# New distances between the moving tiles and the weight blocks in four feed-forward layers

## The chip, the cores and the metric

The program runs on one core of a Trainium2 chip. The metric is the device time of one execution in microseconds; three executions of the kernel before gave 2782.95, 2782.99 and 2783.01 us, median 2782.99 us.

## The reference

Two blocks of a transformer-like network run one after the other on 256 tokens of width 1024. The first block has two layers with a Fourier and a retention mixer; the second has two layers (`l` = 0, 1), each a feed-forward network (ffn), a mixer of state-space, pooling and attention parts, and another ffn. The change is about the four ffns of the second block:

```python
def _swiglu(x, w_gate, w_up, w_down):   # the ffn: 1024 -> 2816 -> 1024
    return (silu(x @ w_gate) * (x @ w_up)) @ w_down
...
    for l in range(DEPTH):
        f = _swiglu(_rmsnorm_2(h, ff1_norm_pre[l]), ff1_w_gate[l], ff1_w_up[l], ff1_w_down[l])
        h = h + 0.5 * _rmsnorm_2(f, ff1_norm_post[l])
        ...
        f = _swiglu(_rmsnorm_2(h, ff2_norm_pre[l]), ff2_w_gate[l], ff2_w_up[l], ff2_w_down[l])
        h = h + 0.5 * _rmsnorm_2(f, ff2_norm_post[l])
```

## The kernel before

All matrix products are made in float32 accuracy out of three products in the faster fp32r type: an operand is split into a high part (rounded to fp32r) and a low part (what was left), and w_hi·hi, w_hi·lo and w_lo·hi are added up in PSUM. `pe_block` (L1182) issues the three matmuls; they are L1193, L1194 and L1195 of every profile row below. Each loads its own block of 128 x 128 weights (PEld, LDWEIGHTS) and then streams a moving tile of 256 token columns (512 in most of the first block) through it.

The weights come from HBM in units of 512 KB into a ring of four slots, `raw` (SP's queue issues them). ACT copies a unit to `w_hi` (`split_hi`, L727), DVE subtracts to get `w_lo` (`split_lo`, L736), and PE consumes the unit. A plan made when the program is built gives each unit its slot; PE waits for `lo_ready` before a unit and counts it off in `unit_used` behind it.

An ffn of the second block (`ffn`, L369) has five steps. "gain" scales the stream `h` into the moving tiles `u_hi` (ACT, `act_gain`, L1688) and `u_lo` (DVE, `dve_gain_tile`, L1695). "up" is a Gemm of 11 turns of 96 matmuls on `u_hi`, `u_lo`; ACT and DVE make g = silu(gate) * up out of it and split it into `g2_hi` (L1080) and `g2_lo` (L1143). "down" is a Gemm of 528 matmuls on `g2_hi`, `g2_lo`. "stats" and "post" normalize and add to `h`. The first two turns of "up" have waits in them, since the token norm is worked out meanwhile; from the third turn to the end of "down", 9 x 96 + 528 = 1392 matmuls, the engine has all it needs ahead of it. This is called the long stretch of an ffn below.

**Where the operands lie.** A partition of SBUF is a row of bytes, and the program lays its buffers one behind another in it. `u_hi`, `u_lo`, `raw`, `w_hi` and `w_lo` follow each other, and each is a whole number of 256 bytes long (4160, 4160, 4 x 1056, 4 x 1088 and 4 x 1088 floats), so they all start at the same place modulo 256. A weight block starts at a multiple of 512 bytes in its slot of 4352 bytes = 17 x 256, so every weight block is at that place too. A moving tile of 256 columns is not:

```python
SHIFT, ROOM = 48, 64
...
        def tokens_at(n, wide=False):
            at = SHIFT if n == SEQ and not wide else 0
            return slice(at, at + n)
```

`tokens_at` (L613) puts it 48 floats, 192 bytes, behind. `g2_hi` and `g2_lo` are in an overlay that starts with `tables` and `poolw` (L461 to 463) and come to the same 192. The distance of the moving tile behind the weight block modulo 256 is called the distance here. The kernel has others too:

- distance 0: the Gemms "q" and "gate" of the retention mixer (`both=True`, 256 columns), and the second half of "pool_v" of the second block's mixer, where the roles are swapped (`pe_tokens_unit`, L1224): the weights move, and the tokens are loaded as blocks.
- distance 192 with swapped roles: the Gemm "v" of the retention mixer.
- distances 64, 96, 128 and 160 in turn: the first half of "pool_v", where a row of the moving tile has 264 columns, 1056 bytes, and starts 32 bytes further on from one k to the next. Its units are laid at the start of the slot (`unit_at`, L618), the tokens 192 behind.
- distance 0 with 512 columns: most of the first block.

In `pe_feature_unit`, `pe_both_pairs` and `pe_tail` the operands come from `operand` (L639). The last ffn of the first block has 256 tokens as well, its tiles are `u_hi`, `g_hi` at distance 192, and the change does not touch it.

Of the kernel before, what the change touches and what calls it, by code (L numbers as in the profile page):

```python
# [19 lines left out]
P = 128  # L20
D = 1024
DT = D // P
SEQ = 256
NTOK = 2 * SEQ
DFF = 2816
FT = DFF // P
# [2 lines left out]
DT_COLS = 8  # L29
KT_MAX = 4  # L30
SHIFT, ROOM = 48, 64
EPS = 1e-6
RET_HEADS, RET_DK, RET_DV = 4, 256, 512
SSD_HEADS, SSD_INNER, SSD_GROUPS = 8, 512, 2
# [259 lines left out]
def build(nc, T):  # L294
# [66 lines left out]
    def block2(l):  # L361
        of_layer = lambda kind, counts: Stage(kind, counts, layer=l)
        w = lambda name: T[name][l]
        wi = w("w_in_2")
        fixed = lambda cols, widths=(UCOLS, UCOLS): (
            lambda it, pair, k0, kt: rows(wi)[:, k0:k0 + kt, cols[pair]:cols[pair] + widths[pair]])
        with_dt = (DT_COLS + UCOLS, UCOLS)

        def ffn(n, pre, post):  # L369
            gate, up = w(f"ff{n}_w_gate_2"), w(f"ff{n}_w_up_2")  # L370
            pick = lambda it, pair, k0, kt: rows((gate, up)[pair])[:, k0:k0 + kt, bass.ds(it * UCOLS, UCOLS)]
            return [Stage("gain", {"uhi": DT, "ulo": DT, "sq": 4, "sum": 4}, gain=(l, pre)),
                    Gemm("up", 11, [4, 4], pick, SEQ, evac="swiglu", k_outer=True, waits="ulo", norm_after=True,
                         wide=False),
                    Gemm("down", 2, [4, 4, 4, 4, 3, 3], in_turn(w(f"ff{n}_w_down_2")), SEQ, act="g", evac="store",
                         waits="g", wide=False),
                    stats(SEQ, half=True), Stage("post", {"post": DT, "px": DT}, gain=(l, post))]
        return ffn(1, "pre1", "post1") + [
            Stage("gain", {"uhi": DT, "ulo": DT, "sq": 4, "sum": 4}, gain=(l, "mix_pre")),
            Gemm("xbc", 2, [4, 4], in_turn(wi, 512), SEQ, evac="to_xbc", k_outer=True, waits="ulo", norm_after=True),  # L380
            Gemm("pool_v", 1, [4, 4], fixed((1536, 2312), with_dt), SEQ, mode="tokens", evac="to_pool_v",
                 widths=with_dt, layer=l),
            Gemm("q_k", 1, [4, 4], fixed((1800, 2056)), SEQ, evac="to_q_k", layer=l),
            of_layer("steps", {}),
            Gemm("z", 1, [4, 4], in_turn(wi, 0), SEQ, evac="to_z", layer=l),
            of_layer("mixer", {"mix_lo": 3}),
            Gemm("mix_out", 2, [4, 4], in_turn(w("w_out_2")), SEQ, evac="store", waits="mix_lo", k_outer=True,
                 last_half_first=True),
            stats(SEQ), Stage("post", {"post": DT, "px": DT}, gain=(l, "mix_post"))
        ] + ffn(2, "pre2", "post2")  # L390
# [6 lines left out]
    with ctx:  # L397
        def overlay(specs):

            with ExitStack() as s:  # L400
                return [s.enter_context(nc.sbuf_tensor(n, shape, dt)) for n, shape, dt in specs]
# [4 lines left out]
        def sem(name):  # L406
# [3 lines left out]
        h = sb("h", [P, DT, NTOK])  # L410
# [48 lines left out]
        rswap = rtab[:, 1536:1664]  # L459

        tab_spec = [("tables", [P, TWO_N], f32), ("poolw", [P, 2 * LAYERS2, P], f32)]  # L461
        tables, poolw, g2_hi, g2_lo = overlay(tab_spec + [
            ("g2_hi", [P, FT, SEQ], f32r), ("g2_lo", [P, FT, SEQ], f32r)])
        (_, _, zs, xpad, cx, pool_u, att_v, qk, xtok, cb, seg, mixf, probs, probs_t,
         small) = overlay([(n + "_", s, d) for n, s, d in tab_spec] + [
             ("zs", [P, 4, SEQ], f32), ("xpad", [P, 8, SEQ + 3], f32), ("cx", [P, 8, SEQ], f32),
# [22 lines left out]
        def lv(l, name, a=0, n=1):  # L489
            at = l * LAYER_N + LAYER_AT[name] + a  # L490
            return lvecs[:, at:at + n]
# [118 lines left out]
        raw_landed = [sem(f"raw_landed{i}") for i in range(RING)]  # L610
        read = (banks01_read, banks23_read)

        def tokens_at(n, wide=False):  # L613

            at = SHIFT if n == SEQ and not wide else 0
            return slice(at, at + n)

        def unit_at(g, cols):  # L618
# [8 lines left out]
        class Order:  # L627
# [5 lines left out]
            def link(self, ins):  # L633
# [2 lines left out]
                ins.then_inc(self.sem, 1)  # L636
                self.eng.wait_ge(self.sem, self.n)

        def operand(g, k):  # L639

            if g.more.get("view") == "ret":
                return [x[:, k, :] for x in (ret_hi, ret_lo)]
            if g.act == "u":
                return [x[:, k, tokens_at(g.tokens, g.more.get("both"))] for x in (u_hi, u_lo)]
            if g.more["wide"]:
                return [x[:, k, tokens_at(g.tokens)] for x in (g_hi, g_lo)]
            return [x[:, k, 0:g.tokens] for x in (g2_hi, g2_lo)]


        def ride_src(group, k):  # L650
# [412 lines left out]
        def act_evacuate(act, g, t, it, pair):  # L1063
            done = read[pair]
            tile2 = bass.ds(it * 4 + 2 * pair, 2)
            if g.evac == "swiglu":
                if pair == 0:
                    if g.norm_after:
                        act.wait_ge(a_normed, it + t["normed"] + 1)
                        act.activation(tmp1[:, :, 0:g.tokens], tmp1[:, :, 0:g.tokens], ACT.Silu).then_inc(done, 1)  # L1070
                    else:
                        complete(act, g, t, it, 0)
                        if begun(it + t["pair"]):
                            act.wait_ge(banks23_read, it + t["pair"])
                        act.activation(tmp1[:, :, 0:g.tokens], blocks(g, it, 0), ACT.Silu).then_inc(done, 1)
                else:
                    act.wait_ge(banks23_read, it + t["pair"] + 1)
                    hi = g_hi if g.more["wide"] else g2_hi
                    at = tokens_at(g.tokens) if g.more["wide"] else slice(0, g.tokens)
                    act.activation(hi[:, bass.ds(it * 2, 2), at], tmp2[:, :, 0:g.tokens],  # L1080
                                   ACT.Copy).then_inc(g_hi_ready, 1)
                return
# [32 lines left out]
        def dve_evacuate(dve, g, t, it, pair):  # L1115
            done = read[pair]
            if g.evac == "swiglu":
# [9 lines left out]
                if pair == 1:  # L1127
# [9 lines left out]
                    dve.tensor_tensor(tmp2[:, :, 0:g.tokens], b, tmp1[:, :, 0:g.tokens], ALU.mult  # L1137
                                      ).then_inc(done, 1)
                    dve.wait_ge(g_hi_ready, it + t["g"] + 1)
                    hi, lo = (g_hi, g_lo) if g.more["wide"] else (g2_hi, g2_lo)  # L1140
                    two = bass.ds(it * 2, 2)
                    at = tokens_at(g.tokens) if g.more["wide"] else slice(0, g.tokens)
                    dve.tensor_tensor(lo[:, two, at], tmp2[:, :, 0:g.tokens],  # L1143
# [540 lines left out]
        def act_gain(act, g, t):  # L1684
            for k in range(DT):
                if begun(t["post"] - DT + k + 1):
                    act.wait_ge(post_ready, t["post"] - DT + k + 1)
                act.activation(u_hi[:, k, tokens_at(SEQ)], h[:, k, 0:SEQ], ACT.Copy, scale=lv(*g.more["gain"], k)  # L1688
                               ).then_inc(u_hi_ready, 1)
                if k % 2 == 1:  # L1690
                    act_square(act, h, SEQ, k // 2, t)

        def dve_gain_tile(dve, g, t, k):
            dve.wait_ge(u_hi_ready, t["uhi"] + k + 1)
            dve.scalar_tensor_tensor(u_lo[:, k, tokens_at(SEQ)], h[:, k, 0:SEQ], lv(*g.more["gain"], k),  # L1695
                                     u_hi[:, k, tokens_at(SEQ)].bitcast(f32), ALU.mult, ALU.subtract
                                     ).then_inc(u_lo_ready, 1)
            if k in (3, 5, 7):
                dve_add_squares(dve, SEQ, k // 2, t)
            if k == 7:  # L1700
                dve_fold_sums(dve, SEQ, 3, t)
# [1040 lines left out]
```

## Time and profile before

| | |
|---|---|
| median of three executions | 2782.99 us (2782.95 to 2783.01) |
| the profiled execution | 2769.7 us |
| its span, first to last instruction | 2767.9 us |
| mean granted TensorE clock | 0.994 of full speed |
| instructions in the span | 45423, of them 18884 matmuls and as many weight loads |

PE is the matmul engine, PEld its weight loads, which run beside matmuls. A matmul's record is longer than the distance from its start to the next one's, since matmuls are pipelined; so the time that a matmul costs is read from starts, or from the number of matmuls in a window. In a window's count the matmuls that began before it and end in it are counted too (one or two).

### The profile page before, as it was taken

The numbers are of one execution on the slowest core, as the hardware profiler recorded it, in microseconds if no ns is written. First come the engines' busy times: TensorE is split into PE (matmuls) and PEld (weight loads), VectorE is DVE, ScalarE is ACT, GpSimd is POOL, SyncE is SP. The second block draws the span as 40 slices with busy tenths as digits, with TensorE's granted clock in tenths as the row PEclk, the third lists the DMA queues.
The fourth block names the chain that finished last, engine by engine and source line by source line (L and its number), as shares of the span: only waits on it lengthen the run. The fifth ranks groups of instructions, "written<-read, shape, count | busy, mean of one in ns | idle before, by whom it ended". The sixth has DMA issues, their size and how long they took to land. (4 is left out here: it accounts for less than half of the span.)

```text
span 2767.9 us, 45423 instructions
## 1 busy us (share of the span) xinstructions
PE 2690.8 (97%) x18884; PEld 2464.0 (89%) x18884; DVE 1690.1 (61%) x2116; ACT 1143.8 (41%) x1464; POOL 0.9 (0%) x13
## 2 busy tenths in 40 slices
PE   7999999999999999999999999999999999999998
PEld 5878898878889888899998999999989999997998
DVE  5774655777325753444447655765876666587764
ACT  5222234522224222225245544544554454455543
POOL 0000000000000000000000000000000000000000
PEclk9999999999999999999999999999999999999999
DMA  8653631466323663544222566566526656662553
GB/s 271 207 182 118 188 114 55 144 186 187 95 93 105 195 193 124 177 130 141 86 84 93 187 192 189 165 209 191 161 66 196 193 169 192 189 175 84 167 179 126
DMA packets 377437, 428.86 MB, mean 155 GB/s; under 512 B 14016, under 2 KB 359488, under 8 KB 377152
## 3 DMA queue, kind: packets, MB, share of 16 engines
q1 hardware_dynamic: 376416, 424.79, 49.7%
q8 instruction: 119, 1.95, 0.3%
q10 hardware_dynamic: 864, 1.80, 0.2%
q14 instruction: 38, 0.31, 0.0%
HBM read 425.49 MB, written 1.05 MB: 154 GB/s over the span
## 5 line engine op out<-in xcount | busy, mean ns | idle before, releaser
L736 DVE TENSOR_TENSOR w_lo<-raw,w_hi 128x1024 fp32r<-128x1024 f32 (+1 forms) x672 | 799.7, 1198 | 811.6 <-ACT w_hi L727 804.5
L727 ACT ACTIVATE w_hi<-raw 128x1024 fp32r<-128x1024 f32 (+1 forms) x672 | 691.1, 1036 | 1025.0 <-PE ps L1195 846.9
L1193 PE MATMUL ps<-u_hi,w_hi 128*128 128x256 f32 (+1 forms) x3168 | 1002.0, 316 | 10.3 <-DVE tmp L1137 5.1
L1195 PE MATMUL ps<-u_hi,w_lo 128*128 128x256 f32 (+1 forms) x3168 | 995.7, 314 | 0.0
L1194 PE MATMUL ps<-u_lo,w_hi 128*128 128x256 f32 (+1 forms) x3168 | 995.6, 314 | 0.0
L1193 PEld LDWEIGHTS ps<-u_hi,w_hi 128*128 128x128 f32 x3168 | 598.6, 189 | 62.2 <-issue 15.6
L1195 PEld LDWEIGHTS ps<-u_hi,w_lo 128*128 128x128 f32 x3168 | 595.6, 188 | 40.0
L1194 PEld LDWEIGHTS ps<-u_lo,w_hi 128*128 128x128 f32 x3168 | 595.8, 188 | 39.6
L1193 PE MATMUL ps<-g_hi,w_hi 128*128 128x256 f32 (+1 forms) x1276 | 399.1, 313 | 0.0
L1195 PE MATMUL ps<-g_hi,w_lo 128*128 128x256 f32 (+1 forms) x1276 | 398.7, 312 | 0.0
L1194 PE MATMUL ps<-g_lo,w_hi 128*128 128x256 f32 (+1 forms) x1276 | 398.7, 312 | 0.0
L1193 PEld LDWEIGHTS ps<-g_hi,w_hi 128*128 128x128 f32 x1276 | 241.0, 189 | 16.6 <-issue 1.2
L1195 PEld LDWEIGHTS ps<-g_hi,w_lo 128*128 128x128 f32 x1276 | 239.5, 188 | 15.4
L1194 PEld LDWEIGHTS ps<-g_lo,w_hi 128*128 128x128 f32 x1276 | 239.6, 188 | 15.3
L808 DVE SCALAR_TENSOR_TENSOR ride_in_g<-raw,cond_cols,ride_in_g 128x1024 f32<-128x1024 f32 x154 | 191.1, 1278 | 0.9 <-DMA raw<-in_w_mod 0.8
L1080 ACT ACTIVATE g_hi<-tmp 128x512 f32 (+2 forms) x88 | 69.8, 793 | 224.8 <-DVE tmp L1137 224.8
L1143 DVE TENSOR_TENSOR g_lo<-tmp,g_hi 128x512 f32 (+2 forms) x88 | 78.5, 892 | 86.5 <-ACT g_hi L1080 86.5
L1224 PE MATMUL ps<-w_hi,u_hi 128*128 128x256 f32 (+1 forms) x320 | 90.6, 283 | 0.0
L1224 PE MATMUL ps<-w_hi,u_lo 128*128 128x256 f32 (+1 forms) x320 | 89.2, 279 | 0.0
L1224 PE MATMUL ps<-w_lo,u_hi 128*128 128x256 f32 (+1 forms) x320 | 89.2, 279 | 0.0
L1327 PE MATMUL ps<-g_hi,w_hi 128*128 128x256 f32 x264 | 75.7, 287 | 0.0
L1201 PE MATMUL ps<-u_hi,w_hi 128*128 128x256 f32 (+1 forms) x256 | 70.7, 306 | 5.1 <-ACT u_hi L1688 5.1
(298 smaller groups left out, 2802.1 us busy)
## 6 DMA issues: line engine op xcount, KB each, us to landing
raw<-in_ffn_w_in SPq DMA_DIRECT2D x176, 512.0 KB, 4.5
raw<-in_w_mod SPq DMA_DIRECT2D x128, 512.0 KB, 4.4
raw<-in_ff_w_gate SPq DMA_DIRECT2D x88, 512.0 KB, 4.4
raw<-in_ff_w_up SPq DMA_DIRECT2D x88, 512.0 KB, 4.3
raw<-in_ffn_w_out SPq DMA_DIRECT2D x64, 512.0 KB, 3.4
raw<-in_ff_w_down SPq DMA_DIRECT2D x64, 512.0 KB, 3.5
raw<-in_ret_w_in SPq DMA_DIRECT2D x48, 512.0 KB, 3.6
raw<-in_w_in SPq DMA_DIRECT2D x36, 512.0 KB, 3.8
```

Source lines behind the costliest of these rows:

```text
L727: act.activation(w_hi[:, slot, unit_at(g, cols)], raw[:, raw_slot, 0:cols], ACT.Copy).then_inc(hi_ready, 1)
L736: dve.tensor_tensor(w_lo[:, slot, at], raw[:, raw_slot, 0:cols], w_hi[:, slot, at].bitcast(f32), ALU.subtract).then_inc(lo_ready, 1)
L808: ins = dve.scalar_tensor_tensor(buffer[:, s, :], raw[:, at % RING, 0:D], cond_cols[:, k, s:s + 1], buffer[:, s, :], ALU.mult, ALU.add)
L1080: act.activation(hi[:, bass.ds(it * 2, 2), at], tmp2[:, :, 0:g.tokens], ACT.Copy).then_inc(g_hi_ready, 1)
L1143: dve.tensor_tensor(lo[:, two, at], tmp2[:, :, 0:g.tokens], hi[:, two, at].bitcast(f32), ALU.subtract).then_inc(g_lo_ready, 1)
L1193: pe.matmul(out, w_hi[:, slot, cols], hi, start=first, stop=False, **check)
L1194: pe.matmul(out, w_hi[:, slot, cols], lo, start=False, stop=False, **check)
L1195: return pe.matmul(out, w_lo[:, slot, cols], hi, start=False, stop=last, **check)
L1201: pe.matmul(out, w_hi[:, slot, cols], hi, start=first, stop=False)
L1224: ins = pe.matmul(out, a, w[:, slot, cols], start=k0 + k == 0 and n == 0 and at == 0, stop=k0 + k == sum(g.ks) - 1 and n == 2, skip_group_ ...
L1327: pe.matmul(half_bank(s, b), w_hi[:, slot, cols], hi, start=k0 + k == 0, stop=False)
```

## The change

Each ffn of the second block gets a `place` of its own, in floats, which is added to where its moving tiles start: -8, 8, -4 and 4 for (layer, ffn) = (0, 1), (0, 2), (1, 1) and (1, 2). The distances become 160, 224, 176 and 208 bytes. `g2_hi` and `g2_lo` become flat buffers with 64 floats, 256 bytes, of room on either side, and `gated2` cuts the tile out of them at 64 + place. Neither the number of instructions nor their order, shapes, waits and transfers change; the mixers and the first block keep their tiles where they were.

```diff
+PLACES = {(0, 1): -8, (0, 2): 8, (1, 1): -4, (1, 2): 4}
...
+            place = PLACES[l, n]
+            return [Stage("gain", {"uhi": DT, "ulo": DT, "sq": 4, "sum": 4}, gain=(l, pre), place=place),
                     Gemm("up", 11, [4, 4], pick, SEQ, evac="swiglu", k_outer=True, waits="ulo", norm_after=True,
-                         wide=False),
+                         wide=False, place=place),
                     Gemm("down", 2, [4, 4, 4, 4, 3, 3], in_turn(w(f"ff{n}_w_down_2")), SEQ, act="g", evac="store",
-                         waits="g", wide=False),
+                         waits="g", wide=False, place=place),
...
-            ("g2_hi", [P, FT, SEQ], f32r), ("g2_lo", [P, FT, SEQ], f32r)])
+            ("g2_hi", [P, FT * SEQ + 2 * ROOM], f32r), ("g2_lo", [P, FT * SEQ + 2 * ROOM], f32r)])
...
-        def tokens_at(n, wide=False):
+        def tokens_at(n, wide=False, place=0):
-            at = SHIFT if n == SEQ and not wide else 0
+            at = SHIFT + place if n == SEQ and not wide else 0
             return slice(at, at + n)
...
+        def gated2(g):
+            at = ROOM + g.more["place"]
+            return [x[:, at:at + FT * SEQ].rearrange("p (k n) -> p k n", n=SEQ) for x in (g2_hi_flat, g2_lo_flat)]
...
-                return [x[:, k, tokens_at(g.tokens, g.more.get("both"))] for x in (u_hi, u_lo)]
+                return [x[:, k, tokens_at(g.tokens, g.more.get("both"), g.more.get("place", 0))] for x in (u_hi, u_lo)]
...
-            return [x[:, k, 0:g.tokens] for x in (g2_hi, g2_lo)]
+            return [x[:, k, 0:g.tokens] for x in gated2(g)]
...
-                act.activation(u_hi[:, k, tokens_at(SEQ)], h[:, k, 0:SEQ], ACT.Copy, scale=lv(*g.more["gain"], k)
+                act.activation(u_hi[:, k, tokens_at(SEQ, False, g.more.get("place", 0))], h[:, k, 0:SEQ], ACT.Copy, scale=lv(*g.more["gain"], k)
```

The writers of `g2_hi` (L1078), `g2_lo` (L1140) and `u_lo` (L1695) take the new places in the same way.

## Rows read from the trace of the kernel before

**Rows 1.** The page: busy time by engine, and the granted clock in 40 slices.

```profile
PE 2690.8 (97%) x18884; PEld 2464.0 (89%) x18884; DVE 1690.1 (61%) x2116; ACT 1143.8 (41%) x1464; POOL 0.9 (0%) x13
...
PEclk9999999999999999999999999999999999999999
```

**Rows 2.** The timeline of PE: first and following matmul of the four long stretches.

```profile
1766.99 0.39 PE L1193 MATMUL ps<-u_hi,w_hi 128*128 128x256 f32 x1 [0.52 <-ACT tmp L1070]
2087.54 0.38 PE L1193 MATMUL ps<-u_hi,w_hi 128*128 128x256 f32 x1 [0.60 <-ACT tmp L1070]
2276.63 0.38 PE L1193 MATMUL ps<-u_hi,w_hi 128*128 128x256 f32 x1 [0.60 <-ACT tmp L1070]
2589.66 0.38 PE L1193 MATMUL ps<-u_hi,w_hi 128*128 128x256 f32 x1 [0.60 <-ACT tmp L1070]
```

**Rows 3.** The timeline of PE: the first matmul behind each of the four long stretches.

```profile
1931.05 0.50 PE L1513 MATMUL ps<-ones,acc 128*128 128x1 f32 x4
2245.41 0.39 PE L1513 MATMUL ps<-ones,acc 128*128 128x1 f32 x3
2434.51 0.39 PE L1513 MATMUL ps<-ones,acc 128*128 128x1 f32 x3
2753.71 0.39 PE L1513 MATMUL ps<-ones,acc 128*128 128x1 f32 x3
```

**Rows 4.** Windows of 150 us: window, us, PE busy (matmuls), clock, DMA share, GB/s.

```profile
1580.00:1730.00 150.00, 150.00 (x1326) 1.00 0.63 194
1770.00:1920.00 150.00, 150.00 (x1276) 1.00 0.65 201
2090.00:2240.00 150.00, 150.00 (x1326) 1.00 0.64 194
2280.00:2430.00 150.00, 150.00 (x1326) 1.00 0.64 195
2592.00:2742.00 150.00, 150.00 (x1276) 1.00 0.60 184
```

**Rows 5.** Groups of weight loads in the window 1768:1930 (busy us, mean ns).

```profile
L1193 PEld LDWEIGHTS ps<-u_hi,w_hi 128*128 128x128 f32 x285 | 54.7, 192 | 0.0
L1195 PEld LDWEIGHTS ps<-u_hi,w_lo 128*128 128x128 f32 x286 | 53.7, 188 | 0.0
L1194 PEld LDWEIGHTS ps<-u_lo,w_hi 128*128 128x128 f32 x285 | 53.5, 188 | 0.0
```

**Rows 6.** Groups of ACT, then of DVE, in windows 1768:1930 and 2090:2240.

```profile
L727 ACT ACTIVATE w_hi<-raw 128x1024 fp32r<-128x1024 f32 (+1 forms) x59 | 60.3, 1024 | 35.8 <-PE ps L1195 35.8
...
L736 DVE TENSOR_TENSOR w_lo<-raw,w_hi 128x1024 fp32r<-128x1024 f32 (+1 forms) x58 | 68.0, 1187 | 43.2 <-ACT w_hi L727 41.9
```

**Rows 7.** Windows at distance 0 (three), then at 192 with swapped roles; columns of rows 4.

```profile
447.50:458.50 11.00, 11.00 (x94) 1.00 0.01 1
1287.00:1309.00 22.00, 22.00 (x185) 1.00 0.47 151
1966.20:1971.60 5.40, 5.40 (x47) 1.00 0.41 106
...
1367.00:1404.00 37.00, 37.00 (x329) 1.00 0.31 98
```

**Rows 8.** The timeline of "pool_v": first of its 48 matmuls of 264 columns, and the next form.

```profile
1960.13 0.28 PE L1224 MATMUL ps<-w_hi,u_hi 128*128 128x264 f32 x1
...
1965.99 0.28 PE L1224 MATMUL ps<-w_hi,u_hi 128*128 128x256 f32 x1
```

**Rows 9.** The page: the writers of the gated tiles.

```profile
L1080 ACT ACTIVATE g_hi<-tmp 128x512 f32 (+2 forms) x88 | 69.8, 793 | 224.8 <-DVE tmp L1137 224.8
L1143 DVE TENSOR_TENSOR g_lo<-tmp,g_hi 128x512 f32 (+2 forms) x88 | 78.5, 892 | 86.5 <-ACT g_hi L1080 86.5
```

**Rows 10.** Two source views: the writers of the moving tiles of "gain" (min/median/max ns).

```profile
L1688 ACT ACTIVATE u_hi<-h,lvecs x48: 507/509/513, 1740.2 to 2572.0; 128x256 fp32r<-128x256 f32 x48
...
  PE ps L1201: 5.1, 6
...
L1695 DVE SCALAR_TENSOR_TENSOR u_lo<-h,lvecs,u_hi x48: 472/476/487, 1740.8 to 2572.5; 128x256 fp32r<-128x256 f32 x48
```

More of the change, by code:

```diff
@@ L371, in ffn @@
             pick = lambda it, pair, k0, kt: rows((gate, up)[pair])[:, k0:k0 + kt, bass.ds(it * UCOLS, UCOLS)]
-            return [Stage("gain", {"uhi": DT, "ulo": DT, "sq": 4, "sum": 4}, gain=(l, pre)),
+            place = PLACES[l, n]
+            return [Stage("gain", {"uhi": DT, "ulo": DT, "sq": 4, "sum": 4}, gain=(l, pre), place=place),
                     Gemm("up", 11, [4, 4], pick, SEQ, evac="swiglu", k_outer=True, waits="ulo", norm_after=True,
-                         wide=False),
+                         wide=False, place=place),
                     Gemm("down", 2, [4, 4, 4, 4, 3, 3], in_turn(w(f"ff{n}_w_down_2")), SEQ, act="g", evac="store",
-                         waits="g", wide=False),
+                         waits="g", wide=False, place=place),
                     stats(SEQ, half=True), Stage("post", {"post": DT, "px": DT}, gain=(l, post))]
@@ L461, in build @@
         tab_spec = [("tables", [P, TWO_N], f32), ("poolw", [P, 2 * LAYERS2, P], f32)]
-        tables, poolw, g2_hi, g2_lo = overlay(tab_spec + [
-            ("g2_hi", [P, FT, SEQ], f32r), ("g2_lo", [P, FT, SEQ], f32r)])
+        tables, poolw, g2_hi_flat, g2_lo_flat = overlay(tab_spec + [
+            ("g2_hi", [P, FT * SEQ + 2 * ROOM], f32r), ("g2_lo", [P, FT * SEQ + 2 * ROOM], f32r)])
         (_, _, zs, xpad, cx, pool_u, att_v, qk, xtok, cb, seg, mixf, probs, probs_t,
@@ L1077, in act_evacuate @@
                     act.wait_ge(banks23_read, it + t["pair"] + 1)
-                    hi = g_hi if g.more["wide"] else g2_hi
+                    hi = g_hi if g.more["wide"] else gated2(g)[0]
                     at = tokens_at(g.tokens) if g.more["wide"] else slice(0, g.tokens)
@@ L1139, in dve_evacuate @@
                     dve.wait_ge(g_hi_ready, it + t["g"] + 1)
-                    hi, lo = (g_hi, g_lo) if g.more["wide"] else (g2_hi, g2_lo)
+                    hi, lo = (g_hi, g_lo) if g.more["wide"] else gated2(g)
                     two = bass.ds(it * 2, 2)
@@ L1694, in dve_gain_tile @@
             dve.wait_ge(u_hi_ready, t["uhi"] + k + 1)
-            dve.scalar_tensor_tensor(u_lo[:, k, tokens_at(SEQ)], h[:, k, 0:SEQ], lv(*g.more["gain"], k),
-                                     u_hi[:, k, tokens_at(SEQ)].bitcast(f32), ALU.mult, ALU.subtract
+            dve.scalar_tensor_tensor(u_lo[:, k, tokens_at(SEQ, False, g.more.get("place", 0))], h[:, k, 0:SEQ], lv(*g.more["gain"], k),
+                                     u_hi[:, k, tokens_at(SEQ, False, g.more.get("place", 0))].bitcast(f32),
+                                     ALU.mult, ALU.subtract
                                      ).then_inc(u_lo_ready, 1)
```

## The prediction

> **What bounds the kernel now.** I read the page first: PE is busy for 2690.8 us of a 2767.9 us span, at the full granted clock in all 40 slices [rows 1]. DVE has 61% and ACT 41%, so an edit counts if it changes how fast matmuls follow each other or how long PE waits. Then the timeline of PE around the four ffns of the second block. Each has a long stretch, 1392 matmuls from the third turn of "up" to the end of "down", with no wait for its operands. The four are the same instructions on the same shapes, and they don't take the same time. From first matmul [rows 2] to the first one behind [rows 3] they last 1931.05 - 1766.99 = 164.06, 157.87, 157.88 and 164.05 us. So two are 6.19 us longer, 6190 / 1392 = 4.45 ns for each matmul. The reader is to see that this is no wait: in windows of 150 us inside the stretches 1324 matmuls start in a fast one (1326 less the two that began before it), one every 113.3 ns, and 1274 in a slow one, one every 117.7 ns, all at clock 1.00, which is the 2.4 GHz level [rows 4]. The last ffn of the first block, whose tiles have distance 192 as well, is fast (first window of [rows 4]).
>
> So at distance 192 there are two spacings, and a stretch that has begun with one holds it to its end. The groups of weight loads show where the difference lies: in a slow stretch every third load takes 192 ns in place of 188 [rows 5]. The others are not late: ACT and DVE idle for 35.8 and 43.2 us before their splits, of windows of 162 and 150 us, ACT waiting for PE to free a slot [rows 6]. Faster matmuls find their weights ready, as the fast stretches show already.
>
> Does the distance matter at all? At distance 0 and the same 256 columns, 92 matmuls start in 11.00 us, 183 in 22.00 and 45 in 5.40: 119.6 to 120.2 ns [rows 7]. "v", with roles swapped at 192, has 327 in 37.00 us, 113.1 ns [rows 7]. At 2.4 GHz 256 columns are 106.7 ns, so a matmul loses 6.6 ns (fast, 192), 11.1 (slow, 192) or 13.3 ns (0). The only rows at distances that are no multiples of 64 bytes are the first half of "pool_v", which goes through 64, 96, 128 and 160: 48 matmuls of 264 columns in 1965.99 - 1960.13 = 5.86 us, 122.1 ns [rows 8]. 264 columns are 110.0 ns, so they lose 12.1 ns. At 256 columns that is an estimate of 118.8 ns.
>
> **The change, part by part.** No instruction, wait or transfer is added or moved. The writers of the tiles (ACT and DVE in "gain", 509 and 476 ns each, 48 of both [rows 10]; 88 splits of g each, 793 and 892 ns on average, with the first block's larger ones among them [rows 9]) write the same elements at a start 16 or 32 bytes away. I cost that at nothing: the g splits are hidden behind the matmuls of the next turn. If a write at such a start took 5% longer, "gain" would lose 8 x 25 ns per ffn, and PE's wait for those tiles, 5.1 us in six times [rows 10], would grow by 4 x 0.2 = 0.8 us at most. Two more buffers' rooms of 512 bytes cost no time.
>
> What is left is the spacing of the four long stretches, 1392 x 4 matmuls, and of 192 matmuls in the first turns of each ffn. The latter stop at waits and pick a spacing anew; 4 x 192 x 4.45 ns = 3.4 us bounds them both ways, and I take 0.
>
> The new spacings are not in the trace; each is bounded by its neighbours, in ns:
> - 160, ffn (0, 1): from 113.3 (192, fast) to 118.8 ("pool_v", whose last quarter it is). I take 118.8, the nearer. The stretch is slow now, so 1.1 x 1392 = +1.5 us.
> - 224, ffn (0, 2): half way from 192 to 256, which is 0; from 113.3 to 120.0. I take 117.7.
> - 176, ffn (1, 1), and 208, ffn (1, 2): 16 bytes on either side of 192; from 113.3 to 118.8 and to 120.0. I take 113.3 for both, as three of the five stretches at 192 hold it.
>
> A spacing below 113.1 stands in no row; 106.7, nothing lost, would be the end, and I leave it out of the range.
>
> **The sum.** Against the profiled execution, 2769.7 us: +1.5 for (0, 1), +6.2 for (0, 2), 0 for (1, 1), -6.2 for (1, 2), so +1.5: 2771.2 us. But the median of the runs is 2782.99, 13.3 us above it. Two more slow stretches would make 2 x 6.19 = 12.4 of that, and nothing else in the rows jumps by such an amount from one execution to another. So I read it as all four changed ffns being slow in the timed runs. Against that, (0, 1) gives +1.5, (0, 2) 0, (1, 1) -6.2 and (1, 2) -6.2: -10.9, so 2772.1 us. Both ways the changed kernel comes out at 2771 to 2772, since it is the spacing behind the change that counts. I forecast 2772.0 us.
>
> **The rivals.** A change of 0.2%, 5.6 us, is about what a measurement of this kernel can tell from none; one stretch that goes over is 6.2 us, just above it.
>
> *Nothing that can be told.* The places do not matter, or as many stretches are slow as before: 2783.0 us, 2777.4 to 2788.6. For it: at one and the same distance the trace has both spacings, so something other than the place picks one, a phase at which a stretch begins behind its last short wait. New places may only draw again. Against it: distance 0 has 120 ns in all three windows and 192 never has [rows 4, 7]. That the tiles do not move as the diff says belongs here too, with a small chance.
> The Trainium skill ("SBUF — State Buffer", section "Who interferes with whom") speaks for this rival: PE has two independent read ports, one for the moving operand and one for weight loads, and it never waits on anyone. By that rule the start of a tile is free and the time stays at 2783. The windows at distances 0 and 192, 120.0 against 113.3 ns for the same shape, do not agree with it, and the measurement decides.
>
> *Slower.* All distances with a spacing under 118 ns are 192, a multiple of 64 bytes, and none of the four new ones is a multiple of 64. If a moving tile that starts inside such a piece costs what "pool_v" and distance 0 lose, 12.1 to 13.3 ns, none of the four stretches can hold the fast spacing any more. At 120.0 in all four, the timed runs with four slow stretches lose 4 x 1392 x 2.3 ns = 12.8 us: 2795.8. If they have two fast ones, as in the profile, it is 2 x 1392 x (2.3 + 6.7) ns = 25.1 us: 2808.1. It decides from a mean spacing of 1.0 ns above the present mean, 5.6 us over 5568 matmuls. For it: the "pool_v" rows, the only ones off the multiples of 64. Against it: they have other columns and change distance every three matmuls, so none of their distances settles.
>
> *Much faster.* All four fast: 2782.99 - 4 x 6.19 = 2758.2 us. It is the far end of my forecast, not a mechanism of its own.
>
> **How the numbers follow.** Faster 0.43: at least two stretches that are slow in the timed runs go fast, or one with little lost elsewhere. Same 0.25. Slower 0.32. I predict 2772.0, the likeliest case. The range takes all four fast, 2758.2, with some of the first turns' 3.4 us, so 2757; upwards it ends at 120 ns in all four, 2795. The 2808 of the worst case is left out, as are places better than any row. Both signs hold much of the chance, so the forecast's own range stands beside it: 2757 to 2777.
>
> **What would show it.** In the changed kernel's trace the windows of 150 us in the four long stretches: some 1263 + 2 matmuls for (0, 1) if 118.8 is right, 1324 + 2 for (1, 1) and (1, 2), 1274 + 2 for (0, 2). The last ffn of the first block stays at 1326. Weight loads of 192 ns: none where it is fast, a third where slow, all at 120 ns as the place nears 0. I am wrong if 176 or 208 runs at 117 ns or more, if spacings differ between a profile and the median of the runs by something else than these stretches, or if ACT's and DVE's writers take longer at the new starts.

## The result, and the profile after

The change makes the kernel slower by 0.6%: the median is 2792.53 us (2788.20 to 2800.23, 11 executions) against 2780.95 us (2763.42 to 2783.01, 11 executions of the kernel before). The ratio is 1.0059, 95% interval 1.0041 to 1.0077, which is 11 to 21 us of 2780.95. The means of the eleven differ by 16.1 us, the medians by 11.6, since six of the eleven times of before lie crowded at 2781 to 2783. The forecast of 2772.0 us had the wrong sign. The profiled execution took 2794.71 us, with a span of 2792.9 us, 25.0 us more than the profiled one of before (2769.7 us).

In the changed kernel the code lies some lines lower: the three matmuls of `pe_block` are L1200, L1201 and L1202 (L1193 to L1195 before).

The page of the changed kernel, busy time by engine. The instruction counts are those of [rows 1]; PE has 27.4 us more.

```profile
PE 2718.2 (97%) x18884; PEld 2488.6 (89%) x18884; DVE 1692.2 (61%) x2116; ACT 1144.7 (41%) x1464; POOL 0.9 (0%) x13
```

The timeline of PE, which answers to [rows 2] and [rows 3]: first matmul of each long stretch and the first one behind it, for the distances 160, 224, 176 and 208.

```profile
1768.20 0.38 PE L1200 MATMUL ps<-u_hi,w_hi 128*128 128x256 f32 x1 [0.53 <-ACT tmp L1077]
1931.63 0.50 PE L1520 MATMUL ps<-ones,acc 128*128 128x1 f32 x4
...
2090.43 0.38 PE L1200 MATMUL ps<-u_hi,w_hi 128*128 128x256 f32 x1 [0.51 <-ACT tmp L1077]
2255.24 0.39 PE L1520 MATMUL ps<-ones,acc 128*128 128x1 f32 x3
...
2286.41 0.38 PE L1200 MATMUL ps<-u_hi,w_hi 128*128 128x256 f32 x1 [0.49 <-ACT tmp L1077]
2452.52 0.28 PE L1520 MATMUL ps<-ones,acc 128*128 128x1 f32 x2
...
2612.69 0.38 PE L1200 MATMUL ps<-u_hi,w_hi 128*128 128x256 f32 x1 [0.47 <-ACT tmp L1077]
2778.67 0.28 PE L1520 MATMUL ps<-ones,acc 128*128 128x1 f32 x2
```

The stretches last 163.43, 164.81, 166.11 and 165.98 us, together 660.33. The rows of before give 164.06 + 157.87 + 157.88 + 164.05 = 643.86. So 16.5 of the 25.0 us lie in the stretches, and the four waits in the brackets show that each starts as before, behind ACT's last piece of the first turns.

Windows of 150 us in the last ffn of the first block (untouched) and in the four stretches, which answer to [rows 4]; us, PE busy (matmuls), granted clock, DMA share, GB/s.

```profile
1580.00:1730.00 150.00, 150.00 (x1326) 1.00 0.63 193
1770.00:1920.00 150.00, 150.00 (x1280) 1.00 0.66 203
2092.00:2242.00 150.00, 150.00 (x1270) 1.00 0.62 186
2288.00:2438.00 150.00, 150.00 (x1260) 1.00 0.61 185
2615.00:2765.00 150.00, 150.00 (x1261) 1.00 0.61 184
```

None of the four comes to the 1326 of a stretch at 113.3 ns. From the starts of the matmuls the mean spacings are 117.33 ns (160), 118.33 (224), 119.26 (176) and 119.17 (208), at clock 1.00 throughout. Each is steady over its stretch.

The groups of weight loads in the same four stretches, one line of each, which answer to [rows 5] (busy us, mean ns).

```profile
L1200 PEld LDWEIGHTS ps<-u_hi,w_hi 128*128 128x128 f32 x288 | 54.1, 188 | 0.7 <-issue 0.7
...
L1200 PEld LDWEIGHTS ps<-u_hi,w_hi 128*128 128x128 f32 x284 | 53.5, 188 | 0.0
...
L1200 PEld LDWEIGHTS ps<-u_hi,w_hi 128*128 128x128 f32 x284 | 54.1, 190 | 0.0
...
L1200 PEld LDWEIGHTS ps<-u_hi,w_hi 128*128 128x128 f32 x282 | 53.3, 189 | 0.0
```

At 160 and 224 the loads take on average the 188 ns that they take where matmuls follow every 113.3 ns, and yet the matmuls are 4 to 5 ns further apart. The time of a load's record is no measure of the loss.

The writers: the page's lines for g, answering to [rows 9], and the source views of the "gain" writers, answering to [rows 10].

```profile
L1087 ACT ACTIVATE g_hi<-tmp 128x512 f32 (+2 forms) x88 | 69.8, 793 | 225.1 <-DVE tmp L1144 225.1
L1150 DVE TENSOR_TENSOR g_lo<-tmp,g_hi 128x512 f32 (+2 forms) x88 | 78.5, 892 | 87.2 <-ACT g_hi L1087 87.2
...
L1695 ACT ACTIVATE u_hi<-h,lvecs x48: 507/509/512, 1741.4 to 2595.0; 128x256 fp32r<-128x256 f32 x48
...
L1702 DVE SCALAR_TENSOR_TENSOR u_lo<-h,lvecs,u_hi x48: 473/479/486, 1742.0 to 2595.6; 128x256 fp32r<-128x256 f32 x48
```

They are the same to 3 ns (u_lo 479 for 476). The new places cost the writers nothing.

**The other 8.5 us** of the profiled execution lie outside the stretches: by the starts above and [rows 2, 3], +1.2 us before the first, +2.3 between (0, 1) and (0, 2), and +5.0 between (1, 1) and (1, 2), nothing elsewhere. The rows show what goes with the last: in the mixer's short dependent steps the granted clock fell to the 1.2 GHz level for a time in this execution, and at the same place in the kernel before it did not. The window of the changed kernel, then the same place in the kernel before:

```profile
2525.00:2545.00 20.00, 17.80 (x67) 0.66 0.03 10
```

```profile
2507.00:2527.00 20.00, 16.83 (x98) 1.00 0.04 15
```

It goes with the execution more than with the distances: a kernel with the same four distances in other ffns (below) has clock 0.91 in its window there, and its profiled execution took 2789.52 us. (The page's row of the clock in [rows 1], which the prediction read as the full clock in all 40 slices, can't show this: a 9 stands for 90% or more of a slice of 69 us.)

### The profile page after: what moved, and what is told of

The parts are those of the page before. It is cut to its first block and busy times, and to the rows that moved or that the text cites. A ratio compares the mean times of both kernels' runs of the same rounds, so it can differ in the third digit from the quotient of the medians.

```text
span 2792.9 us, 45423 instructions
## 1 busy us (share of the span) xinstructions
PE 2718.2 (97%) x18884; PEld 2488.6 (89%) x18884; DVE 1692.2 (61%) x2116; ACT 1144.7 (41%) x1464; POOL 0.9 (0%) x13
## 5 line engine op out<-in xcount | busy, mean ns | idle before, releaser
L1200 PE MATMUL ps<-u_hi,w_hi 128*128 128x256 f32 (+1 forms) x3168 | 1005.3, 317 | 9.2 <-DVE tmp L1144 4.4
L1202 PE MATMUL ps<-u_hi,w_lo 128*128 128x256 f32 (+1 forms) x3168 | 1000.3, 316 | 0.0
L1201 PE MATMUL ps<-u_lo,w_hi 128*128 128x256 f32 (+1 forms) x3168 | 999.4, 315 | 0.0
L1200 PEld LDWEIGHTS ps<-u_hi,w_hi 128*128 128x128 f32 x3168 | 597.6, 189 | 61.2 <-issue 15.3
L1202 PEld LDWEIGHTS ps<-u_hi,w_lo 128*128 128x128 f32 x3168 | 596.6, 188 | 40.1
L1201 PEld LDWEIGHTS ps<-u_lo,w_hi 128*128 128x128 f32 x3168 | 596.8, 188 | 39.3
L1202 PE MATMUL ps<-g_hi,w_lo 128*128 128x256 f32 (+1 forms) x1276 | 401.1, 314 | 0.0
L1200 PE MATMUL ps<-g_hi,w_hi 128*128 128x256 f32 (+1 forms) x1276 | 400.8, 314 | 0.0
L1201 PE MATMUL ps<-g_lo,w_hi 128*128 128x256 f32 (+1 forms) x1276 | 400.6, 314 | 0.0
L1200 PEld LDWEIGHTS ps<-g_hi,w_hi 128*128 128x128 f32 x1276 | 240.4, 188 | 16.7 <-issue 1.2
L1202 PEld LDWEIGHTS ps<-g_hi,w_lo 128*128 128x128 f32 x1276 | 240.0, 188 | 15.6
L1201 PEld LDWEIGHTS ps<-g_lo,w_hi 128*128 128x128 f32 x1276 | 240.1, 188 | 15.1
```

Source lines behind the costliest of these rows:

```text
L1200: pe.matmul(out, w_hi[:, slot, cols], hi, start=first, stop=False, **check)
L1201: pe.matmul(out, w_hi[:, slot, cols], lo, start=False, stop=False, **check)
L1202: return pe.matmul(out, w_lo[:, slot, cols], hi, start=False, stop=last, **check)
```

## The experiments

Three theories were set against each other first. *Distance*: the spacing is decided by how far the moving tile lies behind the weight block. *Start*: it is decided by where the tile itself starts. *Draw*: it is drawn when a stretch begins, and places don't matter. All stretches below are the same 1392 matmuls in the order (0, 1), (0, 2), (1, 1), (1, 2).

### The kernel before, once more

No edit.

> The kernel before, unchanged, for a second trace of it. Three theories. Distance: the spacing of a long stretch follows from the distance of the moving tile behind the weight block alone, and 192 is the one of those seen so far that can hold 113.3 ns. Start: what counts is whether the moving tile itself starts at a multiple of 64 bytes. Draw: each stretch draws one of the spacings where it begins, and the places have no part in it. Distance and start expect the two lengths of before, 157.9 or 164.1 us in each of the four long stretches, and nothing else; if the place alone decided, the same two would be slow again. Draw expects another set of slow stretches.

2772.81 us. Windows of 150 us in its four stretches:

```profile
1772.00:1922.00 150.00, 150.00 (x1276) 1.00 0.66 201
2093.00:2243.00 150.00, 150.00 (x1276) 1.00 0.62 187
2288.00:2438.00 150.00, 150.00 (x1326) 1.00 0.64 195
2601.00:2751.00 150.00, 150.00 (x1326) 1.00 0.60 185
```

The stretches last 164.05, 164.05, 157.88 and 157.88 us. [Rows 4] have them slow, fast, fast, slow; here the order is slow, slow, fast, fast. So at 192 the spacing isn't fixed by the ffn, and it differs between executions of the same program. In both traces two of four were slow, 643.9 us in all.

### Four and eight bytes beside 192

```diff
-PLACES = {(0, 1): -8, (0, 2): 8, (1, 1): -4, (1, 2): 4}
+PLACES = {(0, 1): -1, (0, 2): 1, (1, 1): -2, (1, 2): 2}
```

> The distances are 188, 196, 184 and 200 in the four ffns, 4 and 8 bytes on either side of 192. Distance: if 192 is a sharp point, all four lie between 117.3 and 119.3 ns, 163.4 to 166.1 us; if it is the bottom of a slope, 113.3 ns plus something that grows with the step, 158 to 162 us for 4 bytes. Start: none starts at a multiple of 64, so all four have 117 ns or more, the 4-byte ones no better than the 8-byte ones. Draw: 113.3 or 117.8 in each, 157.9 or 164.1 us.

2796.49 us. Windows of 50 us at 188, in "up" and then in "down":

```profile
1773.00:1823.00 50.00, 50.00 (x435) 1.00 0.64 192
1878.00:1928.00 50.00, 50.00 (x425) 1.00 0.63 195
```

The stretches last 162.54 us (188 bytes), 167.97 (196), 167.14 (184) and 168.59 (200). In "up" and "down" the spacings differ: 115.55 and 118.59 ns at 188, 120.0 and 121.56 at 196, 120.0 in both at 184, 121.68 and 120.0 at 200. One float to either side loses 2.2 to 8.2 ns: 192 is a point, not the middle of a valley. All three expectations missed: no stretch lies in the 163.4 to 166.1 us of a sharp point or has a length of *Draw*, and 115.55 ns is below the 117 that *Start* asked for. That "up" and "down" differ at 188, 196 and 200 has no explanation here; both have the same distance.

### Four quarters

```diff
-PLACES = {(0, 1): -8, (0, 2): 8, (1, 1): -4, (1, 2): 4}
+PLACES = {(0, 1): -48, (0, 2): -32, (1, 1): -16, (1, 2): -24}
```

> The distances are 0, 64, 128 and 96 in the four ffns, three of them multiples of 64. Distance: 120.0 ns at 0 (167 us), and 117 to 122 ns at 64, 96 and 128, as the stretch of 264 columns had them (163 to 170 us). Start: 64 and 128 can hold 113.3 ns, 157.9 us, and 96 can't. Draw: 157.9 or 164.1 us in each.

2802.34 us. Windows of 150 us for the distances 0, 64, 128 and 96:

```profile
1778.00:1928.00 150.00, 150.00 (x1252) 1.00 0.64 197
2100.00:2250.00 150.00, 150.00 (x1276) 1.00 0.62 188
2294.00:2444.00 150.00, 149.52 (x1260) 1.00 0.62 187
2620.00:2770.00 150.00, 150.00 (x1252) 1.00 0.61 185
```

The stretches last 167.13, 164.04, 165.28 and 167.13 us, or 120.00, 117.78, 118.66 and 119.99 ns. The theory that a multiple of 64 bytes is what makes a start fast falls: 0, 64 and 128 are such starts and none has 113.3 here. At distance 0 every weight load takes 192 ns, as the prediction expected. The last ffn of the first block, untouched at 192, had 117.78 ns here (169.73 us, against 163.33 in the trace of before): it is drawn too.

### The weight blocks moved as well

```diff
+PLACES = {(0, 1): 8, (0, 2): 0, (1, 1): 4, (1, 2): 0}
+BLOCKS_AT = {(0, 1): 8, (0, 2): 8, (1, 1): 4, (1, 2): 4}
...
-            at = SHIFT if g.mode == "tokens" and cols <= KT_MAX * UCOLS else 0
+            at = SHIFT if g.mode == "tokens" and cols <= KT_MAX * UCOLS else g.more.get("blocks_at", 0)
...
-            slot, cols = u % RING, slice(k * UCOLS + b * P, k * UCOLS + b * P + P)
+            base = g.more.get("blocks_at", 0) + k * UCOLS + b * P
+            slot, cols = u % RING, slice(base, base + P)
```

Distances 192, 160, 192 and 176, with the blocks 32, 32, 16 and 16 bytes further on.

> The weight blocks move as well. In (0, 1) blocks and tiles are 32 bytes further on and in (1, 1) 16 bytes, so the distance is 192 and nothing starts at a multiple of 64. In (0, 2) and (1, 2) the blocks alone move on, by 32 and 16 bytes, so the distances are 160 and 176 with tiles that start where they did before. Distance: 157.9 or 164.1 us in (0, 1) and (1, 1); 163.4 us in (0, 2), as the tile at 160 had, and 166.1 us in (1, 2), as at 176. Start: (0, 1) and (1, 1) have 163.4 us or more, (0, 2) and (1, 2) 157.9 or 164.1. Draw: 157.9 or 164.1 in each.

2784.79 us. Windows of 150 us in the four stretches:

```profile
1773.00:1923.00 150.00, 150.00 (x1276) 1.00 0.65 200
2096.00:2246.00 150.00, 150.00 (x1281) 1.00 0.62 188
2288.00:2438.00 150.00, 150.00 (x1326) 1.00 0.63 195
2603.00:2753.00 150.00, 149.91 (x1263) 1.00 0.62 188
```

The third line tells most: tile and block both start 16 bytes off, the distance is 192, and the stretch runs at 113.36 ns. With 160 made by moving the block the spacing is 117.33 ns, the number of the changed kernel, whose tile was moved. So the distance between the two operands decides whether 113.3 can be had, and not where either starts. One expectation missed: 176 by the block has 118.67 ns (165.29 us, expected 166.1), and 176 by the tile has 119.26 in two kernels (the changed one, and one below). Either 176 has two spacings or the block's own start has a small part in it; no run separates the two.

### A matmul put in before each unit

At 192 in all four, one extra matmul ahead of each unit (24 matmuls, 18 in the last units of "down"), into an unused PSUM bank, with 32, 64, 128 and 160 columns. If the spacing is held by the chain of matmuls itself, a disturbance moves it from one to the other (*held state*). If it comes from what goes on around the stretch (*surroundings*), it stays.

```diff
+            if "kick" in g.more:
...
+                n = g.more["kick"]
+                pe.matmul(ps[:, RIDE_BANK, 0:n], w_hi[:, u % RING, 0:P], operand(g, k0)[0][:, 0:n], start=True, stop=True)
             for b in range(2):
```

> All tiles at distance 192 as before; ahead of each unit of the long stretches PE gets one more matmul of 32, 64, 128 and 160 columns in the four ffns, on the first block of the unit and the first columns of its tile, into a PSUM bank that nobody uses there. It leaves nothing out. Held state: the spacing is a phase between the stream of moving columns and the weight loads, held from matmul to matmul; an odd matmul shifts it, so the spacing between two kicks is 113.3 in some units and 117.8 in others of the same stretch, or all the same where a kick always leads to one of them. Surroundings: something around the stretch that lasts for all of it (instruction fetch, transfers, the other engines) sets the spacing; then it is one of the two from the first unit to the last, whatever the kick.

2804.55 us, with the extra work. The timeline of PE in the ffn with 128 extra columns; L1244 is the extra matmul.

```profile
2300.12 0.22 PE L1244 MATMUL ps<-u_hi,w_hi 128*128 128x128 f32 x1
...
2300.93 0.28 PE L1201 MATMUL ps<-u_hi,w_hi 128*128 128x256 f32 x1
...
2302.86 0.28 PE L1203 MATMUL ps<-u_hi,w_lo 128*128 128x256 f32 x1
2302.97 0.22 PE L1244 MATMUL ps<-u_hi,w_hi 128*128 128x128 f32 x1
...
2303.79 0.28 PE L1201 MATMUL ps<-u_hi,w_hi 128*128 128x256 f32 x1
...
2305.79 0.28 PE L1203 MATMUL ps<-u_hi,w_lo 128*128 128x256 f32 x1
2305.91 0.22 PE L1244 MATMUL ps<-u_hi,w_hi 128*128 128x128 f32 x1
...
2308.77 0.22 PE L1244 MATMUL ps<-u_hi,w_hi 128*128 128x128 f32 x1
...
2311.70 0.22 PE L1244 MATMUL ps<-u_hi,w_hi 128*128 128x128 f32 x1
```

From the seventh to the last matmul behind the first extra one there are 17 steps in 1.93 us, 113.5 ns; behind the second one the same count takes 2.00 us, 117.6 ns. From one extra matmul to the next it is 2.85, 2.94, 2.86 and 2.93 us in turn. Of the 62 units of this ffn 32 ran at 113.3 to 113.4 and 30 at 117.7 to 117.8 ns, nearly all alternating. With 32 and with 160 columns every fourth unit was fast in the end, with 64 every third. So the spacing is a state of the chain: it lasts until a matmul of another length shifts it. *Surroundings* falls.

### High and low parts at different distances

192 with 64, 192 with 128, 64 with 192 (tile of the high parts, then of the low parts), and in (1, 2) the low weight blocks 64 bytes further on.

```diff
+PLACES = {(0, 1): 0, (0, 2): 0, (1, 1): -32, (1, 2): 0}
+PLACES_LO = {(0, 1): -32, (0, 2): -16, (1, 1): 0, (1, 2): 0}
+BLOCKS_LO = {(0, 1): 0, (0, 2): 0, (1, 1): 0, (1, 2): 16}
...
```

> High and low parts at different distances: in (0, 1) the high tiles are at 192 and the low ones at 64, in (0, 2) at 192 and 128, in (1, 1) at 64 and 192; in (1, 2) the tiles are at 192 and the low weight blocks 64 bytes further on, which makes their pairs 128. Single pairs: if each matmul's loss follows from its own tile and the block that is loaded meanwhile, the spacing is the mean of the three single ones: 113.3 or 117.8 for 192, 117.8 for 64, 118.7 for 128, so 114.8 (159.8 us) at best in (0, 1) and 115.1 (160.3 us) in (0, 2), and 116.3 in (1, 1). Chain: if a loss hands its shift on to the next matmul, the mean does not hold, and the fast spacing is lost as soon as one of three differs: 117 ns or more, 163 us.

2795.12 us; 117.78, 118.73, 117.78 and 118.22 ns, so 164.05, 165.37, 164.05 and 164.66 us. Windows of 150 us in the second and the fourth stretch:

```profile
2100.00:2250.00 150.00, 150.00 (x1265) 1.00 0.62 186
2620.00:2770.00 150.00, 150.00 (x1271) 1.00 0.58 178
```

In the first and third, 117.78 is what 64 has, but also the slow spacing of 192, so by themselves they don't tell much. The second does: two of three distances at 192 and one at 128 have 118.73, where 128 alone has 118.66. The mean would be 115.1 with the fast spacing of 192 and (2 x 117.78 + 118.66) / 3 = 118.07 with the slow one, so here the chain goes at the pace of its worse member. The fourth, also with one of three at 128, has 118.22 and is nearer to the mean with the slow spacing. So these runs don't settle how a mixture finds its pace. None of the four mixtures holds 113.3.

### All four at 64

```diff
-PLACES = {(0, 1): -8, (0, 2): 8, (1, 1): -4, (1, 2): 4}
+PLACES = {(0, 1): -32, (0, 2): -32, (1, 1): -32, (1, 2): -32}
```

> All four ffns at distance 64, where the one stretch seen so far had 117.78 ns, the very spacing of the slow state at 192. Distance alone: 117.8 ns and 164.0 us in all four. Two states there too: at least one of four stretches has 113.3 ns, 157.9 us, if both states are about as likely as at 192.

2793.91 us; 164.04 to 164.05 us in all four, 117.78 ns. In the five stretches at 64 that ran, with the one above, 113.3 never came up. As far as five stretches tell, distance 64 has the slow spacing of 192 only, and 192 can have both.

### A fixed start before each unit

At 192, six matmuls of 256 columns at distance 0 ahead of each unit, and behind them none, or one of 128, 64 or 32 columns.

```diff
...
+                for _ in range(6):
+                    pe.matmul(ps[:, RIDE_BANK, 0:SEQ], block, w_hi[:, u % RING, 0:SEQ], start=True, stop=True)
+                if n:
+                    pe.matmul(ps[:, RIDE_BANK, 0:n], block, operand(g, k0)[0][:, 0:n], start=True, stop=True)
```

> All tiles at distance 192; ahead of each unit of the long stretches PE gets six matmuls of 256 columns whose moving tile is the weight block's own row, distance 0, and then nothing in (0, 1), one matmul of 128 columns at 192 in (0, 2), of 64 in (1, 1), of 32 in (1, 2). Nothing is left out. Held state: distance 0 has one spacing only, 120.0 ns with every load late, so six of them wipe out what was held, and each unit behind them takes the same spacing, in one ffn always 113.3 or always 117.8. Draw: a unit takes either spacing behind the same six matmuls, from unit to unit.

2961.44 us, with the extra work. The timeline of PE: two matmuls of a unit in (0, 1), then the 32-column matmul (L1247) and two matmuls of a unit in (1, 2).

```profile
1791.05 0.28 PE L1203 MATMUL ps<-u_hi,w_lo 128*128 128x256 f32 x1
...
1793.09 0.28 PE L1203 MATMUL ps<-u_hi,w_lo 128*128 128x256 f32 x1
...
2766.72 0.18 PE L1247 MATMUL ps<-u_hi,w_hi 128*128 128x32 f32 x1
...
2767.19 0.28 PE L1201 MATMUL ps<-u_hi,w_hi 128*128 128x256 f32 x1
...
2769.31 0.28 PE L1201 MATMUL ps<-u_hi,w_hi 128*128 128x256 f32 x1
```

Eighteen steps take 2.04 us in the first, 113.3 ns, and 2.12 us in the second, 117.8 ns. It was so in every unit: 62 of 62 fast with none behind the six, 62 of 62 with 128 columns, 62 of 62 with 64, and 62 of 62 slow with 32. Within this execution the same spacing follows from the same start, unit after unit, so *Draw* in the strict sense falls. That executions of the kernel before differ in what the chain was when the stretch began would fit this, but no run shows that start.

### The same four distances in other ffns

```diff
-PLACES = {(0, 1): -8, (0, 2): 8, (1, 1): -4, (1, 2): 4}
+PLACES = {(0, 1): -4, (0, 2): -8, (1, 1): 4, (1, 2): 8}
```

> The four distances of the change, dealt out to other ffns: 176, 160, 208 and 224 in (0, 1), (0, 2), (1, 1) and (1, 2). Distance: the spacings go with the distance: 119.3, 117.3, 119.2 and 118.3 ns, so 166.1, 163.4, 166.0 and 164.8 us. Place in the program: the first stretch has 163.4 us again, the second 164.8, the third and fourth 166.

2789.52 us. 176: 119.26 ns, 160: 118.67, 208: 119.16, 224: 118.33. Three of four keep the changed kernel's spacing in another ffn to 0.01 ns. 160 has 118.67 (165.29 us) where it had 117.33 and 117.33 was expected again, so it has two spacings as 192 does, and neither is near 113.3. *Place in the program* put 166 us on the third and fourth stretch, which fits the third alone (165.97 and 164.82).

### Holding 113.3 in the kernel before

If six matmuls at distance 0 bring the fast spacing about, then one set of them ahead of the long stretch should hold it, for 0.7 us each. The five ffns of 256 tokens get it, the first block's last one among them.

```diff
-            if g.k_major and g.n > 1:
+            if g.evac == "swiglu" and g.tokens == SEQ:
+                turn(1)
+                pe.wait_ge(lo_ready, 2 * g.units + t["unit"] + 1)
+                pe_banks_free(pe, g, t, 2, 0)
+                block, row = w_hi[:, 0, 0:P], w_hi[:, 0, 0:SEQ]
+                for _ in range(6):
+                    pe.matmul(ps[:, RIDE_BANK, 0:SEQ], block, row, start=True, stop=True)
+                turn(2)
+                loop(pe, g, 3, g.n, turn)
+            elif g.k_major and g.n > 1:
```

> The kernel before, and once in each ffn of 256 tokens (the four of the second block and the last of the first), ahead of the third turn and behind its wait, six matmuls at distance 0 into an unused PSUM bank. Held state: all five long stretches have 113.3 ns, in every execution. The long stretches of the second block last 157.9 us, the six matmuls cost 0.7 us each time; from the profiled 2769.7 with two slow stretches this makes 2769.7 - 12.4 + 5 x 0.7 = 2760.8 us, and the executions lie close together, where those of the kernel before went from 2763 to 2783. Draw: spacings of both kinds, and the same spread as before.

Median 2776.06 us (2762.80 to 2786.06, 12 executions) against 2780.23 us (2766.71 to 2793.67, 23 executions of the kernel before): ratio 0.9984, interval 0.9961 to 1.0007, not to be told from no change. The profiled execution took 2763.53 us, and all five stretches in it ran at 113.3 ns behind the six, four of them in these windows:

```profile
1770.00:1920.00 150.00, 150.00 (x1326) 1.00 0.68 208
2085.00:2235.00 150.00, 150.00 (x1325) 1.00 0.64 194
2274.00:2424.00 150.00, 150.00 (x1325) 1.00 0.64 195
2589.00:2739.00 150.00, 150.00 (x1324) 1.00 0.61 188
```

This one execution looks as *Held state* expected, but five fast of five can be chance. In the other traces 5 of 10 untreated stretches at 192 in the second block were fast and 9 of 12 in the first block's last ffn; at those odds five of five come up about once in 21 executions. That every execution would have 113.3 fails by an estimate. Take a trace's span, and take off the 1392 matmuls that end each of the five ffns: what is left is 1966.3 to 1974.8 us in the twelve traces without a matmul ahead of each unit (2767.9 - 643.9 - 157.8 = 1966.3 in the kernel before). So the part outside differs by 8.5 us, while the twelve times here go up to 2786.06, 22.5 us above the profiled one. By this estimate at least 14 us of that lie in the long stretches, which is more than two slow ones at 6.2 us. The mean granted clock doesn't explain it: 2779.06 us had 0.991, as the profiled 2763.53 did. So six matmuls ahead of a stretch don't fix the time of the kernel. No trace shows why the six, which set 62 units of 62 above, did not.

With four matmuls in place of six (the `range` is the only difference):

> The same with four matmuls in place of six, which is about where the spacing reached 120 ns behind a fast unit. Held state, wiped out in four: 2759.6 us and close together. If four are too few, some stretch takes 117.8 ns and 6.2 us more.

Median 2777.89 us (2769.88 to 2785.05), ratio 0.9991, interval 0.9970 to 1.0011. In its profiled execution (0, 1) and (1, 2) went on at 113.33 ns, (0, 2) and (1, 1) at 117.78. Four don't settle the chain, and two slow of four is also what the kernel before had in both its traces.

### Four more distances

```diff
-PLACES = {(0, 1): -8, (0, 2): 8, (1, 1): -4, (1, 2): 4}
+PLACES = {(0, 1): -40, (0, 2): 12, (1, 1): -12, (1, 2): 20}
```

> The changed kernel with distances 32, 240, 144 and 16 in the four ffns. Distance: none holds 113.3 ns; 117 to 121 ns in all four, 163 to 168 us. Otherwise 192 is not alone, and some of them has 157.9 us.

2785.01 us. 32: 117.78 ns; 240: 117.14; 144: 118.67; 16: 116.67, a little below the 117 expected. With these, 17 distances were run in a long stretch, and 192 alone held 113.3 ns in any of them. Next to it come 188 (115.55, in "up" only) and 16. Most of the others ran in one to three stretches, so a fast spacing that one of them takes now and then could have been missed.

## Why the prediction was wrong

**The step that failed** is "176, ffn (1, 1), and 208, ffn (1, 2): [...] I take 113.3 for both, as three of the five stretches at 192 hold it". It took the nearest row's spacing to hold 16 bytes away. The runs show 113.3 at the distance 192 itself and nowhere beside it: 176 has 119.26 ns, 208 has 119.17. That is (119.26 + 119.17 - 2 x 113.3) x 1392 = 16.5 us more than taken. The prediction's own bounds for 176 and 208 reached to 118.8 and 120.0 (176 lies above its bound), and the only rows off the multiples of 64 bytes, "pool_v" at 118.8 [rows 8], stood at that end. The choice went by the nearest place where the spacing should have gone by whether any row beside 192 was fast. None was. The measured 2792.53 us lies inside the stated range, but near the end that stood for 120 ns in all four.

**Terms of the sum**, against the profiled execution: (0, 1) at 160 was put at +1.5 us and measured -0.6 (163.43 against 164.06); (0, 2) at 224 at +6.2, measured +6.9; (1, 1) at 176 at 0, measured +8.2; (1, 2) at 208 at -6.2, measured +1.9. Predicted +1.5, measured +16.5, so 15.0 us off: the two terms taken at 113.3 were 8.2 and 8.1 us too low, the other two 1.4 us too high together.

**The second step that failed** is the reading of the median: "So I read it as all four changed ffns being slow in the timed runs". Two more slow stretches do make 12.4 us, and that may be what these three runs had; they have no trace. But it was taken for the kernel's lasting condition, and it isn't one: eight further runs spread from 2763.42 to 2782.45 us, and the two traces of before have two slow stretches of four each, not the same two. Against such draws the four new spacings cost 660.33 - 643.86 = 16.5 us, inside the 11 to 21 us of the measured ratio. Against four slow stretches (4 x 164.05 = 656.2) they would cost 4.1 us. That "the changed kernel comes out at 2771 to 2772" both ways held by its arithmetic, and failed with the 113.3. The profiled execution was a low base besides: outside its five stretches it has 1966.3 us, the least of the twelve traces compared above. So the right spacings put on it give 2769.7 + 16.5 = 2786.2 us, still 6.3 below the measured median.

**The rivals.** *Slower* came in, by another mechanism than the one it named. Starts off the multiples of 64 bytes aren't the cause: 0, 64 and 128 are slow as well, and a tile and a block that both start 16 bytes off are fast if 192 bytes lie between them. Its condition, a mean 1.0 ns above the present one, was met: (660.33 - 643.86) us / 5568 = 2.96 ns. *Nothing that can be told* was half right about the kernel before, where a phase picks one of two spacings; it was wrong that new places only draw again, since none of the new ones drew the fast spacing in the two or three stretches that each had.

The Trainium skill ("TensorE: Matmul & The Clock Gate", section "Step-by-step: what each phase is for") says that loading the next weights doesn't take SBUF read bandwidth from the running matmul. By that the place of one operand behind the other should cost nothing, and these runs don't agree: the same matmul with the same load at the same clock takes 113.3 to 121.7 ns where nothing but that distance was changed. What in SBUF or in the engine makes the distance count stays open; no row here sees inside either.

**What was right:** that PE's spacing is the bound and reaches the end (16.5 us in the stretches, 11 to 21 us by the ratio's interval; that the ratio itself gives 16.4 is closer than it can be trusted); that the distance sets the spacing; that the writers cost nothing; that distance 0 has 120.0 ns; that a stretch at 192 or at one of the four new distances holds its spacing to its end (at 188, 196 and 200 "down" took another than "up"). The sign of weight loads of 192 ns, "a third where slow", was wrong: 160 and 224 are slow and their groups of loads keep a mean of 188.

**Still open:** why a stretch at 192 begins one way in one execution and the other way in the next. The executions of before in one comparison lie 27 us apart (2766.71 to 2793.67). Four stretches going over make 24.8 us and the first block's last ffn 6.4 us more, while all that is outside them differed by 8.5 us in the twelve traces (1966.3 us at a mean granted clock of 0.994, 1974.6 and 1974.8 at 0.989 and 0.990). So most of the 27 us are slow stretches, by an estimate from traces of other executions. No measured version beats the kernel before by more than can be told.

## What to carry to other kernels

Where a chain of matmuls with a fresh weight load each is the bound, compare the spacing from start to start in equal stretches, and try the places of the two operands relative to each other one by one. A good place can be a single point, so the neighbour's value is no estimate, and a spread over neighbours loses it. Where the time of an unchanged program spreads, take a second profile before one reading of the first is made the base of a sum.

## What the runs showed of the hardware that was not expected

- One shape (fp32r, 128x128 weights, 256 moving columns) runs at 113.3 to 121.7 ns at clock 1.00 by the distance of its operands modulo 256 bytes. (The ring's slots lie 17 x 256 bytes apart and the blocks 512, and the spacing is steady over them.) Of 17 distances only 192 reached 113.3; 0, 96 and 184 have 120.0, 200 has up to 121.7.
- At 192 the chain has two steady spacings, 113.33 and 117.78 ns. One odd matmul between units moves it from one to the other, and six matmuls at distance 0 ahead of each unit set it to the first in 62 units of 62 in one execution. Once ahead of a stretch, six did not fix the time over twelve executions, and four left two of five ffns slow.
- The weight load's record doesn't carry the loss: a mean of 188 ns at spacings of 113.3, 117.3 and 118.3 ns alike. All loads have 192 at distance 0 (120.0 ns), while at 96, with 120.0 ns too, the three groups have 188, 190 and 187.
- A chain of mixed distances did not hold 113.3 in any of four stretches, though two of three distances were 192 in three of them. One went at the pace of its worse member (192 and 128: 118.73, 128 alone: 118.66), another nearer to the mean of the slow spacings (118.22 against 118.07).
